# Sums of squares by TensorE and two key units moved, in a two-block transformer kernel

## What is computed

```
silu_c, silu_cc = silu(c), silu(c_ctx)
mod_l = split(silu_c  @ w_mod + b_mod, 6)      # w_mod: 2048 x 12288
mod_c = split(silu_cc @ w_mod + b_mod, 6)
hl = rms_norm(x,   norm1_g) * (1 + mod_l[1]) + mod_l[0]
hc = rms_norm(ctx, norm1_g) * (1 + mod_c[1]) + mod_c[0]
zl  = hl @ w_in + b_in                          # w_in: 2048 x 13312
zkv = hc @ w_in[:, K_OFF:G_OFF] + b_in[K_OFF:G_OFF]
```

## Time and profile before

| | |
|---|---|
| median of 3 runs | 2831.27 us (2827.95 to 2837.47) |
| the profiled execution's own time | 2836.03 us |
| its span in the profile | 2834.1 us |
| mean granted clock of TensorE | 0.977 |
| busy: PE, DVE, ACT, POOL | 2707.5, 1917.5, 1271.6, 222.6 us |
| L563, PE waiting for POOL in the first 200 us | 9.3 us, 2 times |
| L591, PE waiting for ACT in the first 200 us | 8.0 us, 2 times |
| L530, PE waiting for DVE in the first 200 us | 6.7 us, once |

### The profile page before, as it was taken

One profiled execution on the slowest core, in us unless ns is written; L12 is line 12 of the kernel. 1 busy time (PEld: TensorE's weight loads), 2 busy tenths in 40 slices (PEclk: granted clock), 3 DMA queues, 4 the chain that ended last, 5 costly groups with the idle time before them and its releaser, 6 DMA issues.

```text
span 2834.1 us, 51449 instructions
## 1 busy us (share of the span) xinstructions
PE 2707.5 (96%) x21378; PEld 2579.3 (91%) x21378; DVE 1917.5 (68%) x2951; ACT 1271.6 (45%) x1851; POOL 222.6 (8%) x212
## 2 busy tenths in 40 slices
PE   5989999899999899999999999999999998979996
PEld 2579977799999899999999999999999998979996
DVE  4845667789999787885554555677656665477564
ACT  4522244544434545543443444464444444444453
POOL 4000001100004100100000000030000000220011
PEclk7999999999999999999999999999999999989998
DMA  7756643365778687776555555554444443535563
GB/s 272 278 188 208 227 128 117 106 207 185 262 238 258 206 279 260 253 258 212 188 184 187 185 184 187 183 192 149 158 133 157 149 156 110 188 107 178 185 195 111
DMA packets 163991, 539.02 MB, mean 190 GB/s; under 512 B 31024, under 2 KB 35120, under 8 KB 163632
## 3 DMA queue, kind: packets, MB, share of 16 engines
q1 hardware_dynamic: 163760, 535.73, 56.9%
HBM read 533.57 MB, written 2.10 MB: 189 GB/s over the span
## 4 chain that ended last, share of the span: by engine, by line
PE 61%; DVE 5%; issue 1%; ACT 1%; POOL 0%; POOLq 0%; ACTq 0%; DVEq 0%
PE ps L525 19%; PE ps L530 19%; PE ps L527 19%; DVE lo L1558 1%; DVE row L2127 1%; PE ps L852 0%; DVE AL L2203 0%; PE ps L874 0%; PE ps L875 0%; DVE H L2211 0%; PE ps L563 0%; DVE ON L2135 0%; DVE Z L2291 0%; PE ps L947 0%; PE ps L946 0%
## 5 line engine op out<-in xcount | busy, mean ns | idle before, releaser
L973 ACT ACTIVATE hi<-raw 128x1024 fp32r<-128x1024 f32 x856 | 900.5, 1057 | 961.6 <-PE ps L530 466.7
L525 PE MATMUL ps<-AH,hi 128*128 128x256 f32 (+2 forms) x4480 | 1284.1, 287 | 13.5 <-DVE AL L2203 13.5
L530 PE MATMUL ps<-AH,lo 128*128 128x256 f32 (+2 forms) x4480 | 1271.3, 284 | 16.5 <-DVE lo L1558 16.4
L527 PE MATMUL ps<-AL,hi 128*128 128x256 f32 (+2 forms) x4480 | 1269.6, 283 | 0.0
L1558 DVE TENSOR_TENSOR lo<-raw,hi 128x1024 fp32r<-128x1024 f32 x856 | 1037.4, 1225 | 211.4 <-ACT hi L973 209.0
L525 PEld LDWEIGHTS ps<-AH,hi 128*128 128x128 f32 x4480 | 849.5, 190 | 45.6 <-issue 33.8
L530 PEld LDWEIGHTS ps<-AH,lo 128*128 128x128 f32 x4480 | 851.5, 190 | 19.3 <-DVE lo L1558 19.2
L527 PEld LDWEIGHTS ps<-AL,hi 128*128 128x128 f32 x4480 | 850.3, 190 | 1.0
L525 PE MATMUL ps<-YH,hi 128*128 128x256 f32 (+1 forms) x1536 | 435.2, 283 | 6.5 <-DVE YL L2138 6.5
L530 PE MATMUL ps<-YH,lo 128*128 128x256 f32 (+1 forms) x1536 | 434.2, 283 | 0.0
L527 PE MATMUL ps<-YL,hi 128*128 128x256 f32 (+1 forms) x1536 | 433.9, 283 | 0.0
(11 more groups left out here) (248 smaller groups left out, 2485.0 us busy)
## 6 DMA issues: line engine op xcount, KB each, us to landing
raw<-in_w_ff SPq DMA_DIRECT2D x256, 512.0 KB, 4.2
raw<-in_w_in SPq DMA_DIRECT2D x208, 512.0 KB, 4.5
raw<-in_w_mod SPq DMA_DIRECT2D x192, 512.0 KB, 4.7
raw<-in_w_ain SPq DMA_DIRECT2D x128, 512.0 KB, 3.6
raw<-in_w_pin SPq DMA_DIRECT2D x64, 512.0 KB, 3.6
raw<-in_w_o SPq DMA_DIRECT2D x32, 512.0 KB, 4.7
raw<-in_w_aout SPq DMA_DIRECT2D x32, 512.0 KB, 3.5
raw<-in_w_pout SPq DMA_DIRECT2D x32, 512.0 KB, 4.2
```

Source lines behind the costliest of these rows:

```text
L525: e.matmul(b.ap[:, o], hi[:, k, :], xh, start=start and k + i == 0, stop=False, skip_group_check=many)
L527: e.matmul(b.ap[:, o], hi[:, k, :], xl, start=False, stop=False, skip_group_check=many)
L530: mm = e.matmul(b.ap[:, o], los[j % NSPLIT][:, k, :], xh, start=False, stop=stop and k == KU - 1, skip_group_check=many)
L973: e.activation(his[u % NSPLIT][:, :, :], raws[raw_at[i]][:, :].rearrange("p (k m) -> p k m", k=KU), ACT.Copy).then_inc(s_hi, 1)
```

## The change

ScalarE squares x and ctx in four pieces of four tiles each, into memory of their own (`squares`), and TensorE sums all 16 tiles of a norm by 16 fp32 matmuls with the 1/2048 matrix into one bank: x's behind unit 6, ctx's behind unit 10. GpSimd does nothing for these two norms. Both roots stand behind all squares on ScalarE. In the list of units, eight w_mod units instead of four follow each key unit, so the first halves of columns 40 and 41 are units 48 and 57, and those of 42 and 43 are units 66 and 67, behind the last w_mod unit, 65. Key units now tick on all three engines, and the last block's copy and turn come one tick earlier, the turn between units 66 and 67. VectorE makes the second part of unit 68 and the products of unit 69 (w_mod) ahead of `finish`. SP issues two w_mod blocks ahead of x that it issued behind it, one of them ahead of cst.

```diff
-SQ = dict(x=0, ctx=16, sgv=32, cv=40, n2=48, s=64, on=96, z=112, pin=128, z2=144)
-ADD = dict(x=0, ctx=16, sgv_m=32, sgv=40, cv_m=48, cv=56, n2=64, s=80, on=112, z=128, pin=144, z2=160)
+SQ = dict(sgv=0, cv=8, n2=16, s=32, on=64, z=80, pin=96, z2=112)
+ADD = dict(sgv_m=0, sgv=8, cv_m=16, cv=24, n2=32, s=48, on=80, z=96, pin=112, z2=128)
...
@@ unit_plan
-    share = (64 - NEARLY) // NLEAD
     for j in range(NLEAD):
         plan.append(("w_in", 40 + j, 0))
-        plan += mod0[NEARLY + share * j:NEARLY + share * (j + 1)]
+        plan += mod0[NEARLY + 8 * j:NEARLY + 8 * j + 8]
...
@@ split_times
     ahead(FIRST - 1, use + AHEAD)
+    dve[FIRST - 1] += later[:AHEAD - 1]
+    done.update(later[:AHEAD - 1])
+    del later[:AHEAD - 1]
...
@@ build
-        extra = []
+        extra, under, upon = [], [], []
...
-            sb(f"under{i}", [128, 12 * T], F32, over)
+            under.append(sb(f"under{i}", [128, 12, T], F32, over))
...
-            sb(f"over{i}", [128, 12 * T], F32, first, "right")
+            upon.append(sb(f"upon{i}", [128, 12, T], F32, first, "right"))
...
+        squares = [two[j // 3][:, 4 * j % 12:4 * j % 12 + 4, :] for two in (under, upon) for j in range(4)]
...
@@ sync
-            for _ in range(2):
+            for _ in range(3):
                 block_in()
             e.dma_start(cst[:, :], ar["cst"]).then_inc(s_cst, 16)
+            block_in()
             e.dma_start(H[:, :, NM:L], ar["x"]).then_inc(s_x, 16)
             for _ in range(4):
                 block_in()
             e.dma_start(ctxv, ar["ctx"]).then_inc(s_ctx, 16)
-            for _ in range(NSTART + NRAW - 6):
+            for _ in range(NSTART + NRAW + len(dve_at[FIRST - 1]) - 8):
                 block_in()
...
@@ tensor
             def norms():
-                for key in ("x", "ctx"):
-                    for _ in range(8):
+                for c, key in enumerate(("x", "ctx")):
+                    for _ in range(6 - 3 * c):
                         yield
-                    mean(key, 2048, T, last=ADD[key] + 16)
-                    yield
-                    for _ in range(4):
-                        yield
+                    opened(xb)
+                    for k in range(16):
+                        if k % 4 == 0:
+                            e.wait_ge(s_sqx, 4 * c + k // 4 + 1)
+                        mm = e.matmul(XB[:, 0:T], ones[2048][:, :], squares[4 * c + k // 4][:, k % 4, :],
+                                      start=(k == 0), stop=(k == 15))
+                    mm.then_inc(s_mean, 1)
+                    xb.free = (s_root, MEAN[key] + 1)
+                    yield
 
             def mod0_turn(r):
                 yield
-                yield
+                if r < 7:
+                    yield
...
                     unit(b, 0, both, True, False, lambda k: e.wait_ge(s_lx, 2 * k + 2))
+                    tick()
                     continue
...
@@ scalar
                 for key, src, s_in in (("x", H[:, :, NM:L], s_x), ("ctx", ctxv, s_ctx)):
                     e.wait_ge(s_in, 16)
-                    for k in range(16):
-                        square(src[:, k, :], T)
-                        if k % 2:
-                            yield
+                    for j in range(4):
+                        at = MEAN[key] * 4 + j
+                        e.activation(squares[at], src[:, 4 * j:4 * j + 4, :], ACT.Square).then_inc(s_sqx, 1)
+                        yield
+                for key in ("x", "ctx"):
                     root(rows[ROW[key] % 2], T)
-                    yield
-                    for k in range(4):
+                    for _ in range(4):
                         yield
-                    have.add(key)
+                have.add("ctx")
 
             def mod0_out(r, nb):
-                yield
+                if r < 7:
+                    yield
...
@@ scalar, vector
-                if name == "w_in":
-                    continue
-                if q == 7:
+                if name != "w_in" and q == 7:
...
@@ vector
                     r = rows[ROW[key] % 2]
-                    for _ in range(8):
+                    for _ in range(8 if key == "x" else 1):
                         yield
...
@@ gpsimd
-            norm("x", 16, T)
-            norm("ctx", 16, T)
```

More of the change, by code:

```diff
@@ L359, in build @@
             sem(f"s_{n}") for n in ("tanh", "silu", "lamp", "lam", "lame", "setup"))
-        s_m0p, s_m0e, s_m0t, s_m0v, s_mx, s_hx, s_lx, s_cs = (
-            sem(f"s_{n}") for n in ("m0p", "m0e", "m0t", "m0v", "mx", "hx", "lx", "cs"))
+        s_m0p, s_m0e, s_m0t, s_m0v, s_mx, s_hx, s_lx, s_cs, s_sqx = (
+            sem(f"s_{n}") for n in ("m0p", "m0e", "m0t", "m0v", "mx", "hx", "lx", "cs", "sqx"))
         s_k, s_vf, s_vt, s_vtok, s_q, s_mask, s_qk, s_bias, s_max, s_exp, s_pn, s_ptr, s_pta, s_ptv, s_av, s_na = (
@@ L1018, in norms, with mod0_out @@
                     e.wait_ge(s_in, 16)
-                    for k in range(16):
-                        square(src[:, k, :], T)
-                        if k % 2:
-                            yield
-                    root(rows[ROW[key] % 2], T)
-                    yield
-                    for k in range(4):
-                        yield
-                    have.add(key)
-            def mod0_out(r, nb):
-                yield
+                    for j in range(4):
[3 more added lines that the diff above has]
+                for key in ("x", "ctx"):
+                    root(rows[ROW[key] % 2], T)
+                    for _ in range(4):
+                        yield
+                have.add("ctx")
+            def mod0_out(r, nb):
+                if r < 7:
+                    yield
                 e.wait_ge(s_unit, unit_no["mods", nb, 7] + 1)
```

## The result

The changed kernel takes 2808.15 us (median of 4 runs, 2807.37 to 2812.01), the kernel before beside it 2832.76; the ratio is 0.9916, with a 95% interval of 0.9896 to 0.9936. Two further comparisons of the unaltered changed kernel gave 0.9907 (0.9894 to 0.9920) and 0.9896 (0.9879 to 0.9912). It is faster, by 25 to 28 us in the medians; 2807 was forecast. The profiled execution took 2808.74, against 2836.03 before.

The account below looks back on a forecast made before the run. TensorE, busy 96% of the span, was taken to bound the kernel, so only its waits and slow clock could be won. Stretches of -0.6, +13.6 and +11.1 us sum to 24.1: median 2831.27 to 2807, range 2796 to 2821.

Parts of the forecast that it names:

- First stretch: Up to unit 11: GpSimd wait of 7.97 us replaced by two sums, start 52.1 against 51.52, -0.6 us.
- the price of a sum: Each norm's 16 fp32 matmuls on TensorE: 7.8 us at full clock, 8.3 starting slow; bounds 7 and 15.
- A sum's weight loads: Loads of 128 fp32 columns in the sums: taken as hidden, though the skill's rule spoke against it; bare would mean 2813.
- rival (c): Loads of ones bare in the sums: ctx's sum takes 13.4 to 15 us instead of 8.3, result 2813; chance 0.07.
- Second stretch: Unit 11 to unit 48: 49.6 us of work plus 4.6, 54.2 us; unit 48 starts at 106.3, +13.6 us.
- one slow window behind these waits: Between units 11 and 48, behind VectorE's waits of 2 and 0.8 us: one low-clock place costing 1.8 us.
- Rival (b): Middle gives nothing: VectorE holds TensorE, each wait brings a slow window; only 12 us won, 2819; chance 0.20.
- signs of being wrong in the middle: Between units 11 and 48: wrong if unit 48 comes after 112 or granted clock there is under 0.9.
- Third stretch: Unit 48 to end of unit 68: waits 3.39 and 6.68 and slow clock 1.7 go, less 0.7: +11.1 us.
- Behind unit 68: From the end of unit 68 to the end: same work in the same order, costed at nothing.
- Rival (d): Time won is lost to waits further on, key units starved of their blocks: 2831; chance 0.06.
- Rival (e): Slower: TensorE's clock stays at 1.2 GHz through units 11 to 47, costing 44.6 us against 24.1 won: 2852; chance 0.05.

Follow-up runs that it names:

- part 3 alone: Kernel before with only the second part of unit 68 and products of unit 69 made ahead of the last modulate group: 2827.04 us, ratio 0.9981.
- the parts alone: Kernel before given only the sums on TensorE and new loading order, 2821.17 us; or only the new unit order, ticks, earlier turn 7 and early second part, 2821.26.
- part 1 alone: Changed kernel with old unit order, no ticks at key units, turn 7 in its old place and second parts as before: 2821.17 us, ratio 0.9956.
- without part 3: Changed kernel with the second part of unit 68 behind the last modulate group again: 2813.31 us, ratio 0.9921.
- x doubled: Changed kernel with the sum for x made twice, 16 fp32 matmuls more: 2809.62 us, ratio 0.9916.
- ctx doubled: Changed kernel with the sum for ctx made twice: 2815.67 us, ratio 0.9934.
- the lead of three: Changed kernel with VectorE's second parts made three units ahead of TensorE, not two, in the first 68 units: 2812.71 us, ratio 0.9919.
- both last edits: Changed kernel with idle ticks in modulate's first two groups, and ctx's sum in its own bank ahead of turn 0: 2805.14 us, ratio 0.9889.

## Why the prediction was right, step by step

- **First stretch** (forecast -0.6 us, measured +1.4, and +1.8 and -0.3 in the two further executions). The mechanism held: block 8 landed at 28.8 (28.4 forecast), turn 0 came at 38.9 (38.5), x's sum was free, ctx's on the path. The term that was mis-sized is the price of a sum: 7.1 us with the tail of its last matmul and 6.8 to the next start, not 7.8 to 8.3. The 1.94 us of the earlier trace rows hold the tail of the last of four matmuls, and the prediction counted it once in every four. The turn and unit 10 also ran 0.9 us faster than was allowed for, as the clock rose at 43; in the execution with -0.3 it rose only at 46, inside ctx's sum, which took 8.0 us.
- **A sum's weight loads.** They are hidden at 128 columns too: 0.22 us a record with its load. The Trainium skill's rule that fp32 weights get no fast load (TensorE: Matmul & The Clock Gate, Weight-path perf modes) had no consequence here, and rival (c) falls.
- **Second stretch** (54.2 us forecast, measured 59.4 and 59.7, and 51.9 in a third execution). The work alone was right: 49.6 forecast, 49.3 in the execution without a slow place. The waits near 70 were forecast as 2.0 and measured as 1.97; those near 96 as 0.8, measured 1.83. The step that failed is "one slow window behind these waits": there were two in two executions and none in the third. Of the 7.5 us between the first and the third 1.2 are waits, so the two slow places are worth 6.2, where 1.8 was forecast for one. Rival (b) named the right mechanism, a wait and then low clock; it took 5.2 us of the stretch's gain, where it was to take all but a little. One of the prediction's own signs of being wrong in the middle, a granted clock under 0.9, was there (0.88 from 50.14 to 109.50, and 1.00 in the third execution); the other, unit 48 after 112, wasn't.
- **Third stretch** (51.0 us forecast, measured 49.9). Both waits and the slow clock gone, and the 0.7 us that the third block of second parts was to cost didn't come. The last group was ready 8.2 us behind turn 7; forecast 8.7. The prediction's aside, that 3.3 us would show without unit 67, is worked out wrongly: unit 68 would then want the last k tile at 4.8, so 3.9. In part 3 alone, where no unit 67 stands between, no wait showed: the group wasn't delayed there, and a low clock stretched unit 68 itself to 7.2 us.
- **Behind unit 68** (nothing forecast, 5.2 us measured between the two profiled executions). This step failed as a statement on single executions, see below. By the end of unit 68 the change had won 22.0 us of the 24.1 forecast; that the medians differ by 24.6 is in part this remainder.
- **The number.** That 2807 was met within 1.2 us is in part luck. Against the forecast the three stretches of the profiled execution were off by +2.0, -5.2 and +1.1 us of gain, and 5.2 us that no term of the sum has came from behind unit 68.
- **Rival (d)** falls with the parts alone: of the 13.6 us won in front 12.4 passed through the tail. **Rival (e)** falls with the windows: between units 11 and 48 the granted clock is 0.50 only in two places, from 70.3 to 77.1 and from 97.6 to 104.4, and 1.00 in the rest. What the Trainium skill says of the low clock as the state from which activity releases (TensorE: Matmul & The Clock Gate, What's actually happening) agrees with 0.57 at 39 to 43 behind an idle 36 to 39 and 1.00 from 43.

## What to carry to other kernels

Before a reduction is moved to the bound engine, look at which of its instances stands in a wait that something else sets: of two equal sums of 7.1 us one was free and one was on the path, and the trace of before was enough to tell which. Two fixes of one wait don't add: the value of each depends on whether the other is there, so test each alone and each taken out. And a copy or a turn that must follow one unit is best issued behind that unit and ahead of work that waits for loads, with a unit of pure matrix work between it and the next consumer.

## What the runs showed that was not expected

**The same waits bring a slow clock or don't.** With waits of 0.72 and 1.25 us near 70, the whole unit behind took 3.58 us in one execution of the changed kernel and 1.88 in another. With the slow place near 97, that made 51.9 us or 59.4 of this stretch. Seven profiled executions (three of the changed kernel, and those of part 1 alone, without part 3, x doubled and ctx doubled) have this pair of waits, the same to 0.02 us: in six the whole unit behind took 2.92 to 3.58 us, in one 1.88. Near 96 the waits themselves differ: with 1.83 and 2.06 us in two executions there was a slow place behind, with 0.60 to 1.36 in the other five none. Two cases are too few for a rule, and why the same pair acts differently is open.

**Matmuls ran at two paces at full granted clock.** In the stretch behind the attention of the first block, the same matmuls run at 179 records in 20 us in one kernel and at 172 in another. Windows of the changed kernel and of the one with x's sum doubled, with the columns of the earlier trace rows, each 190 us behind the first matmul of the attention's products:

```profile
536.60:556.60 20.00, 20.00 (x179) 20.00 (x178) 19.64 (x32) 10.91 (x13) 0.00 (x0) 1.00 0.78 254
```

```profile
531.50:551.50 20.00, 20.00 (x172) 20.00 (x171) 19.32 (x31) 9.95 (x12) 0.00 (x0) 1.00 0.81 246
```

Both show a granted clock of 1.00 and a TensorE without pause. The pace holds for some 80 us and costs 3 us. That stretch was slow with x doubled, ctx doubled, the lead of three, without part 3 and with both last edits, and fast in the other nine executions. Such stretches come elsewhere too: the kernel before ran at 172 from 200 to 240, just behind the change. From the end of unit 68 to the end of the span all 14 executions run the same matmuls, and they take 2644.2 to 2654.1 us; the kernel before has 2652.7, the changed one 2647.5, 2644.8 and 2645.9. The first 1400 matmul records behind unit 68 took 162.4 us in the kernel before and 160.3 in each of the other 13 executions, so 2.1 of the 5.2 us lie there, right behind the change, and they came with every edit, part 3 alone too. The kernel before was profiled only once, so whether the change makes the fast pace likelier or it fell so is open; what sets the pace wasn't tried.
